# Turning the rows of each routing-list tile in a mixture-of-experts decoder layer

## The reference

```python
scores = jax.nn.sigmoid((h @ w_router).astype(jnp.float32))      # 64 experts
...                                                              # best 4 of 8 groups, then
_, eidx = lax.top_k(jnp.where(emask, sel, -jnp.inf), TOP_K)      # 8 experts for each token
hg = jnp.einsum('td,edf->tef', h, w_gate_e)                      # 1024 -> 256
hu = jnp.einsum('td,edf->tef', h, w_up_e)
act = jax.nn.silu(hg) * hu * gates[..., None]
routed = jnp.einsum('tef,efd->td', act, w_down_e)                # 256 -> 1024
shared = (jax.nn.silu(h @ w_gate_sh) * (h @ w_up_sh)) @ w_down_sh
```

## Time and profile before

| | us |
|---|---|
| median of three runs | 1099.96 (1099.4 to 1100.63) |
| the profiled execution, its own time | 1099.3 |
| its span, first to last instruction | 1097.5 |
| PE busy in the span | 934.3 (85%) |
| DVE busy | 404.1 (37%) |
| POOL busy | 242.0 (22%) |
| ACT busy | 202.2 (18%) |

### The profile page before, as it was taken

One profiled execution on the slowest core, in us unless ns is written; L12 is line 12 of the kernel. 1 busy time (PEld: TensorE's weight loads), 2 busy tenths in 40 slices (PEclk: granted clock), 3 DMA queues, 4 the chain that ended last, 5 costly groups with the idle time before them and its releaser, 6 DMA issues.

```text
span 1097.5 us, 13692 instructions
## 1 busy us (share of the span) xinstructions
PE 934.3 (85%) x4773; PEld 440.3 (40%) x4773; DVE 404.1 (37%) x975; ACT 202.2 (18%) x415; POOL 242.0 (22%) x301
## 2 busy tenths in 40 slices
PE   4979987997988889799899897899797979999784
PEld 3564555465534544333333332333232324333231
DVE  5957447857873652123111111111111111111116
ACT  6050031141213131111111110111110111111103
POOL 1910029002300166102111211112111210222012
PEclk9989998998999899899899998999898999999988
DMA  9720120231226118899999999999999999999945
GB/s 325 304 77 5 74 78 0 77 90 70 47 79 231 46 55 346 359 377 385 394 381 384 385 389 392 376 381 374 370 394 382 372 374 376 359 339 388 381 147 195
DMA packets 66421, 289.66 MB, mean 264 GB/s; under 512 B 17291, under 2 KB 18539, under 8 KB 41392
## 3 DMA queue, kind: packets, MB, share of 16 engines
q1 hardware_dynamic: 45376, 250.21, 57.7%
q0 software_dynamic: 13232, 35.04, 12.2%
q10 hardware_dynamic: 7744, 3.53, 1.2%
HBM read 257.14 MB, written 41.18 MB: 272 GB/s over the span
## 4 chain that ended last, share of the span: by engine, by line
PE 47%; issue 29%; DVE 13%; ACT 5%; DMA 4%; ACTq 1%; SPq 0%; POOL 0%; DVEq 0%; POOLq 0%
PE bank L998 24%; PE bank L1944 21%; DVE arena L1592 3%; DVE arena L698 2%; PE bank L1036 2%; DMA prm<-expert_lists 1%; DVE arena L800 1%; ACT arena L1265 1%; DMA sum_rows<-arena,xs 1%; ACT arena L1252 1%; DVE bb L720 1%; DMA qkv_samples<-arena 1%; DVE arena L1923 1%; DMA arena<-in_x_prompt 1%; DVE arena L1905 1%
## 5 line engine op out<-in xcount | busy, mean ns | idle before, releaser
L998 PE MATMUL bank<-arena 128*32 128x512 f32 (+6 forms) x2930 | 539.7, 601 | 82.2 <-issue 52.9
L998 PEld LDWEIGHTS bank<-arena 128*32 128x32 f32 (+3 forms) x2930 | 198.3, 132 | 391.1 <-issue 376.4
L1944 PE MATMUL bank<-arena 128*128 128x512 f32 (+9 forms) x1208 | 309.2, 444 | 32.7 <-ACT arena L1549 8.5
L1944 PEld LDWEIGHTS bank<-arena 128*128 128x128 f32 (+4 forms) x1208 | 173.0, 191 | 162.3 <-issue 128.8
L465 POOL DMA_INDIRECT arena<-h_rows,xs x42 | 43.6, 1039 | 466.7 <-DVE bb L720 455.3
L698 DVE SCALAR_TENSOR_TENSOR arena<-arena,xs,bank 128x256 f32<-128x256 f32 x42 | 27.7, 660 | 312.1 <-issue 271.5
L695 DVE COPY arena<-bank 128x512 f32<-128x512 f32 x41 | 28.4, 692 | 179.1 <-PE bank L998 174.6
L554 ACT ACTIVATE arena<-bank 128x256 f32<-128x256 f32 x42 | 16.1, 383 | 328.7 <-PE bank L998 284.2
L474 POOL DMA_INDIRECT sum_rows<-arena,xs x41 | 64.6, 1576 | 53.4 <-DVE arena L695 30.6
L1592 DVE TENSOR_TENSOR arena<-arena 64x512 f32<-64x512 f32 (+8 forms) x79 | 68.3, 865 | 6.5 <-DMA arena<-o_samples 3.8
L484 POOL DMA_INDIRECT expert_lists<-arena,ncim x40 | 39.8, 994 | 91.4 <-issue 87.7
(11 more groups left out here) (231 smaller groups left out, 529.1 us busy)
## 6 DMA issues: line engine op xcount, KB each, us to landing
arena<-in_w_gate_e SPq DMA_DIRECT2D x64, 1024.0 KB, 18.4
arena<-in_w_up_e SPq DMA_DIRECT2D x64, 1024.0 KB, 34.5
arena<-in_w_down_e SPq DMA_DIRECT2D x64, 1024.0 KB, 33.8
arena<-in_w_in SPq DMA_DIRECT2D x5, 2048.0 KB, 9.0
expert_lists<-arena SPq DMA_DIRECT2D x1, 8482.5 KB, 28.9
arena<-in_x_prompt SPq DMA_DIRECT2D x8, 512.0 KB, 5.9
arena<-in_w_out SPq DMA_DIRECT2D x2, 2048.0 KB, 8.3
arena<-sum_rows SPq DMA_DIRECT2D x8, 512.0 KB, 7.9
```

What stands on the lines that cost most here:

```text
L998: return nc.tensor.matmul(o, l, r, start=start, stop=stop, skip_group_check=True)
L1944: return nc.tensor.matmul(o, l, r, start=start, stop=stop, skip_group_check=True, **kw)
```

## The change

Each list tile gets a number n in the order of the plan. Its rows no longer begin at its first place: the list is turned by k = 11 n mod 16 places (0, 11, 6, 1, 12, ...) and goes around at the tile's end. The empty places of a tile, which stood at its end, now lie somewhere within it. What is computed for each row is the same, in another place of the tile.

A turned list is fetched by two transfers, of width - k rows and of k rows. Only where k is 0 it stays one. So 110 list transfers become 213, with widths like 53 and 11, or 31 and 1. The expert's number is loaded once for tiles of one rank in a row, where before each tile loaded it. A table of constants (`c_unit`) and the count of landings follow.

```diff
+def turned(u):
+    parts = []
+    for n, (r, c0, width, first) in enumerate(UNITS[u]):
+        k = 11 * (TILES_BEFORE[u] + n) % 16
+        parts.append((r, c0 + k, width - k, first))
+        if k:
+            parts.append((r, c0, k, first + width - k))
+    return parts
+
+TILES_BEFORE = [sum(len(t) for t in UNITS[:u]) for u in range(NU)]
 def lists_landed(u):
-    return 16 * sum(len(UNITS[w]) for w in range(u % LISTS, u + 1, LISTS))
+    return 16 * sum(len(turned(w)) for w in range(u % LISTS, u + 1, LISTS))
...
-            for r, c0, width, first in UNITS[u]:
-                e = act.value_load(order_i[0:1, r:r + 1], min_val=0, max_val=NE - 1)
+            e, known = None, None
+            for r, c0, width, first in turned(u):
+                if r != known:
+                    e, known = act.value_load(order_i[0:1, r:r + 1], min_val=0, max_val=NE - 1), r
                 act.dma_start(lists[u % META][c0:c0 + width, :],
...
+        for r_, c0, width, first in turned(u):
+            unit[c0:c0 + width, u] = first + np.arange(width)
         for r_, c0, width, first in tiles:
-            unit[c0:c0 + width, u] = first + np.arange(width)
```

## The result

| | before | after |
|---|---|---|
| median of four runs, us | 1099.68 (1097.96 to 1100.63) | 1150.0 (1148.92 to 1151.6) |
| span of the profiled execution, us | 1097.5 | 1149.4 |
| PE busy, us | 934.3 | 938.0 |

The changed kernel takes 1.0461 times as long (95% interval 1.0441 to 1.0480). The prediction was 1153. In the changed kernel's profile the lines of the code stand 16 further down: the list transfers are L397, the up and down products L1014, `pe_act` L1052, the gating L714, the first step of the meta L734.

A forecast was written before the change was run, and what follows sets the result against it. PE and the weight transfers were taken to share the bound. 1099.3 us + 82 (late lists) + 22 (clock) + 8.5 (start) - 59 (weight waits and their clock) = 1152.8, predicted 1153; own range 1116 to 1182, 8-in-10 range 1090 to 1185.

The forecast's parts named there:

- Equal shares: List transfers: rows split equally over the largest divisor of the width up to 16 engines, beginning at the same engine.
- even cut: Rival, list transfers: odd widths dealt over all 16 engines, rounded up; 1092 us (chance 0.08) or 1079 (0.05), together 0.13.
- shares on changing engines: Rival, list transfers: equal shares, but each transfer starts on another engine; four units stay late, 1118 us, chance 0.06.
- Late lists: Expert loop: 19 lists exceed the packets their deadline allows on the first engine; DVE and PE stand, +82 us.
- sign (a): DMA issues: median list landings of close row counts lie far apart, 53 rows near 20 us, 52 near 6.
- Sign (b): DVE in the loop: waits for `expert_lists` at L718's successor rise from near zero to some 80 us.
- The clock: PE in the loop: gaps from thirteen lists late by 2 us or more each cost clock, 1.7 us apiece, +22 us.
- Weight waits: PE in the loop: weights catch up while PE stands for lists, so weight waits and their clock go, -59 us.
- covered lists: Rival, loop: late lists fall in units where PE would have waited for weights anyway; 1108 us, chance 0.05.
- The start: Ahead of the loop: the third list lands later and delays the first up product, +8.5 us, between 0 and 12.
- ACT's issues in the loop: ACT in the loop: eight transfers with two loads take 4.7 us, over before the next silu; cost 0.
- The turn's worth: Token rows in the loop: evening out rows over engines is worth between nothing and 59 us; forecast unaffected.

The follow-up runs named there:

- e1: Changed kernel's cut into the same widths, but rows left in the places of the kernel before; 1157.2 us, 1.053 times the kernel before.
- e10: Changed kernel with the turn in units 0 to 3 alone and ACT's shared-expert copies and last silu between the four lists; 1102.4 us.
- e4: Changed kernel with turn step 12 instead of 11, so all widths are multiples of 4; 1094.4 us, 0.997 times the kernel before.
- e2: Changed kernel with each piece cut again into a multiple of 16 and a remainder, 316 transfers; 1098.3 us, 1.0005 times the kernel before.
- e8: Changed kernel with expert weights fetched in twice as many transfers, packets of 4 KB instead of 8 KB; 1119.7 us, 1.019 times the kernel before.

## Why the prediction held, step by step

**Equal shares** (the choice on which the rest stands) held exactly: 7660, 9392 and 8086 packets. The even cut falls with it. The shares on changing engines have the same counts and fall by the lateness: they leave four lists late and 1118 us, and 19 lists were late and the kernel took 1150.

**Late lists.** 82 us forecast from 19 late lists; DVE waited 19 times for lists in the loop, and PE 14 times, 80.2 us. (13 places were forecast, counted with 48 packets for every list; the limits that give the 82 us make it 15.) The mechanism is right, that the sum fits so well was partly luck. The packets came 0.33 us apart in the place above, and at that price the same working makes 113 us, an estimate. On the other side, it let every list packet wait for a weight packet, while the weights run out of free slots behind a wait. And the deadlines were worked out as if ACT's issues never stood, and in the changed kernel some did, for up to 5.3 us. My sign (a) stays unread, since no view of the changed kernel gives the lists' landings by row count. Sign (b) was put wrongly: DVE's waits for lists come to far more than 80 us, since DVE would have stood idle for PE in most of that time. PE's side is the one that costs.

```profile
DVE xs L734 <- DMA prm<-expert_lists: 178.3, 19, 15.7
```

**The clock** behind the gaps: 22 us forecast, and the 19.6 us behind the weight waits to go, so +2.4. PE's busy time grew by 6.5 in the loop. The term was too small by 4.1, and the forecast had nothing for the end (+3.5) and the first part of the execution (-1.3); the lists' term was too large by 5.6 (76.4 more at `pe_act` than before, for 82) and the start's by 2.0. These nearly cancel.

**Weight waits** -39.6 us: gone, as forecast; *covered lists*, which had them stay in part, falls. That it happens whatever the turn does is shown by e1, which has no turn and no weight waits.

**The start** came to 6.5 us for 8.5, the first up product at 472.40 for 476, and the step was told with half of its cause. The third list's lateness was real (5.1 us in e10). But ACT's block, which I priced at +3.5 us and called covered, grew by 11.1: six more transfers at 0.8 us (e4's five took 4.03 more), not 0.38, and 6.2 us in two issues that stood. It ended last.

**ACT's issues in the loop** cost nothing by their number in the changed kernel, as forecast: eight took 4.68 us from 599.33, for 4.7, and the silu behind them began at 605.44, when PE was done. With up to twelve for a unit, in e2, they do cost: 9.0 us.

**The turn's worth** stood open between nothing and 59 us; in e4 it is 2.6 us in the loop, and in e2 it can't be told from the cost of the issues. In the even-cut rival I had taken 0.50 us for each row less on the fullest engine and the clock on top; measured was 0.39 with the clock.

## What to carry to other kernels

Before cutting a transfer, look at the divisors of its widths: 53 rows are 53 packets on one engine, 52 are 4. Price a small transfer by the packets on its fullest engine times its own packet and that of whatever else the engine is moving, and hold that against its deadline. If rows have to be turned or shifted, do it by multiples that keep 16 or at least 4 engines, and choose them by which places share an engine.

## What the runs showed of the hardware that was not expected

An engine's issue can stand. A list transfer normally takes ACT 0.33 us to issue; in the changed kernel the longest took 5.48 us (line L397: ns, least, median, most):

```profile
L397 ACTq DMA_DIRECT2D prm<-expert_lists  x213: 234/326/5477, 438.7 to 1076.5; - x107
```

The longest ones follow directly on pieces of 58 and 59 rows, and the standing piece itself was tiny: 6 rows at 442.79, 5 rows (5.3 us) at 702.09. In the block ahead of the loop e2 issued 19 transfers with 57 packets for the first engine, and none took over 0.6 us; in the changed kernel the piece that stood came after 91 had been issued for it, less what had been moved by then. With weight packets of half the size (e8) the same thirteen issues took at most 0.86 us each, and the block shrank to 13.13 us. So it isn't the number of transfers that makes the issuer stand; a backlog on one engine fits all three kernels. At how many packets it begins, no run settles.

And a profile's releaser is only the last of several: e10 took away the wait that it named, 13 us long, and gained 1.3 us.
